# Down-projection weights loaded as four adjacent rows a partition, activations transposed by every fourth column

## The reference

```
def swiglu(h, w1, w3, w2):
    a = silu(einsum('bsd,df->bsf', h, w1)) * einsum('bsd,df->bsf', h, w3)   # 1024 -> 3584
    return einsum('bsf,fd->bsd', a, w2)                                     # 3584 -> 1024, the down projection
```

## Time and profile before

| | |
|---|---|
| median of 3 runs | 1467.38 us (1467.17 to 1470.71) |
| the profiled execution: its own time | 1469.89 us |
| its span, from the first to the last instruction | 1468.1 us |
| PE busy | 1448.4 us (99%), 7542 matmuls |
| DVE busy / ACT busy | 1143.0 us (78%) / 951.2 us (65%) |
| DMA | 439.30 MB, mean 299 GB/s |

### The profile page before, as it was taken

One profiled execution on the slowest core, in us unless ns is written; L12 is line 12 of the kernel. 1 busy time (PEld: TensorE's weight loads), 2 busy tenths in 40 slices (PEclk: granted clock), 3 DMA queues, 4 the chain that ended last, 5 costly groups with the idle time before them and its releaser, 6 DMA issues.

```text
span 1468.1 us, 19713 instructions
## 1 busy us (share of the span) xinstructions
PE 1448.4 (99%) x7542; PEld 1205.7 (82%) x7542; DVE 1143.0 (78%) x968; ACT 951.2 (65%) x844; POOL 35.6 (2%) x22
## 2 busy tenths in 40 slices
PE   8999999999999999999999999999999999999998
PEld 7998888888886788887888888888888888888886
DVE  6984764454476798978888988888898889898886
ACT  7643543443476766767786777777777777677674
POOL 0000000000000000000000001000000000000000
PEclk9999999999999999999999999999999999999999
DMA  9510665544442499999999999999999999999994
GB/s 349 214 58 10 250 216 213 201 171 145 173 163 83 155 362 371 380 358 369 379 359 397 387 367 375 391 364 369 395 391 362 384 375 362 395 390 375 370 370 170
DMA packets 184384, 439.30 MB, mean 299 GB/s; under 512 B 4880, under 2 KB 6416, under 8 KB 184336
## 3 DMA queue, kind: packets, MB, share of 16 engines
q1 hardware_dynamic: 180496, 426.11, 78.6%
q0 software_dynamic: 2848, 10.49, 2.4%
q10 hardware_dynamic: 992, 2.05, 0.4%
HBM read 432.34 MB, written 6.29 MB: 299 GB/s over the span
## 4 chain that ended last, share of the span: by engine, by line
PE 76%; issue 8%; DMA 8%; DVE 6%; ACT 2%; POOL 0%; DVEq 0%; SPq 0%; POOLq 0%; ACTq 0%
PE ps L268 23%; PE ps L270 23%; PE ps L269 23%; DMA raw<-in_od_moe_w 7%; DVE wlo L257 3%; ACT whi L251 1%; PE ps L446 1%; DMA out<-arena,slot_tok 1%; PE ps L974 1%; PE ps L1171 0%; PE ps L873 0%; PE ps L2079 0%; DVE hTlo L312 0%; DVE small L1401 0%; PE ps L329 0%
## 5 line engine op out<-in xcount | busy, mean ns | idle before, releaser
L257 DVE TENSOR_TENSOR wlo<-raw,whi 128x2048 fp32r<-128x2048 f32 x406 | 906.1, 2273 | 167.3 <-ACT whi L251 165.0
L251 ACT CAST whi<-raw 128x2048 fp32r<-128x2048 f32 x406 | 750.7, 1899 | 222.9 <-DMA raw<-in_od_moe_w 162.3
L268 PE MATMUL ps<-whi,hThi 128*128 128x512 f32 (+1 forms) x1240 | 490.1, 395 | 0.0
L270 PE MATMUL ps<-whi,hTlo 128*128 128x512 f32 (+1 forms) x1240 | 482.8, 389 | 0.0
L269 PE MATMUL ps<-wlo,hThi 128*128 128x512 f32 (+1 forms) x1240 | 482.0, 389 | 0.0
L270 PEld LDWEIGHTS ps<-whi,hTlo 128*128 128x128 f32 x1240 | 233.2, 188 | 49.1
L268 PEld LDWEIGHTS ps<-whi,hThi 128*128 128x128 f32 x1240 | 233.5, 188 | 47.5 <-issue 1.2
L269 PEld LDWEIGHTS ps<-wlo,hThi 128*128 128x128 f32 x1240 | 233.6, 188 | 45.7 <-issue 0.2
L268 PE MATMUL ps<-whi,aThi 128*128 128x512 f32 x560 | 219.4, 392 | 0.5 <-DVE wlo L257 0.5
L270 PE MATMUL ps<-whi,aTlo 128*128 128x512 f32 x560 | 218.5, 390 | 0.0
L269 PE MATMUL ps<-wlo,aThi 128*128 128x512 f32 x560 | 218.1, 389 | 0.0
(11 more groups left out here) (308 smaller groups left out, 783.7 us busy)
## 6 DMA issues: line engine op xcount, KB each, us to landing
raw<-in_od_moe_w SPq DMA_DIRECT2D x168, 2048.0 KB, 9.8
raw<-in_ev_ffn_w SPq DMA_DIRECT2D x21, 2048.0 KB, 7.8
raw<-in_ev_w_in SPq DMA_DIRECT2D x6, 2048.0 KB, 12.8
raw<-in_ev_w_out SPq DMA_DIRECT2D x2, 2048.0 KB, 8.6
raw<-in_od_w_in SPq DMA_DIRECT2D x2, 2048.0 KB, 7.8
raw<-in_od_w_out SPq DMA_DIRECT2D x2, 2048.0 KB, 8.1
raw<-in_ev_w_in SPq DMA_DIRECT2D x2, 1024.0 KB, 8.4
xres<-in_x SPq DMA_DIRECT2D x2, 512.0 KB, 4.6
```

Of the source, the lines that this page charges most:

```text
L251: act.copy(whi[s][:, part], raw[s][:, part]).then_inc(hi_ready, 1)
L257: dve.tensor_tensor(wlo[s][:, part], raw[s][:, part], whi[s][:, part].bitcast(F32), ALU.subtract).then_inc(lo_ready, 1)
L268: pe.matmul(to, lhi, rhi, start=first, stop=False)
L270: return pe.matmul(to, llo, rhi, start=False, stop=last)
```

## The change

The rows of a w2 unit are split as (p c) in place of (c p). Partition p then holds rows 4p, 4p+1, 4p+2 and 4p+3, which are one piece of 16 KB in HBM; slice c is rows c, c+4, c+8 and so on. To match, block c of the transposed activations is every fourth column of `actf`, from column c. The transposes read their stationary operand with a step of four elements. Nothing else is changed: the same number of DMAs, bytes, transposes and matmuls, in the same order, with the same waits.

```diff
-        w2f = a["ev_ffn_w2"][0].rearrange("(b c p) n -> b p c n", p=P, c=FC)
+        w2f = a["ev_ffn_w2"][0].rearrange("(b p c) n -> b p c n", p=P, c=FC)
         w1m, w3m = (a[n][0].rearrange("e (k p) n -> e p k n", p=P) for n in ("od_moe_w1", "od_moe_w3"))
-        w2m = a["od_moe_w2"][0].rearrange("e (b c p) n -> (e b) p c n", p=P, c=FC)
+        w2m = a["od_moe_w2"][0].rearrange("e (b p c) n -> (e b) p c n", p=P, c=FC)
...
         def pe_turn(pe, g):
             pe.wait_ge(a_ready, g + 1)
+            by_block = actf.rearrange("p t (i c) -> p t c i", c=FC)
             for c in range(FC):
-                ins = pe.transpose(TP[0][:, c * P:c * P + P], actf[:, 0, c * P:c * P + P], ident)
+                ins = pe.transpose(TP[0][:, c * P:c * P + P], by_block[:, 0, c], ident)
             ins.then_inc(aT_ps, 1)
...
             def turn(i, banks=H1):
 
+                by_block = actf.rearrange("p t (i c) -> p t c i", c=FC)
                 for t in range(TT):
                     pe.wait_ge(a_ready, 2 * i + t + 1)
                     for c in range(FC):
-                        ins = pe.transpose(banks[t][:, c * P:c * P + P], actf[:, t, c * P:c * P + P], ident)
+                        ins = pe.transpose(banks[t][:, c * P:c * P + P], by_block[:, t, c], ident)
                     ins.then_inc(aT_ps, 1)
```

## The result

The changed kernel takes 1476.18 us at the median (21 runs, 1469.0 to 1479.68) against 1467.38 us for the kernel before (21 runs, 1463.8 to 1474.79). The ratio is 1.0041, with a 95% interval of 1.0029 to 1.0053: some 6 us slower (the ratio is that of the means; the medians are 8.8 us apart), where 20.6 us were forecast. That is under a third of the forecast by the ratio and under a half by the medians. Run again beside later experiments it gave 1.0036 (1.0015 to 1.0056) and 1.0048 (1.0034 to 1.0062). The profiled execution took 1473.8 us, its span is 1471.9 us.

A forecast was written before the change was run, and what follows sets the result against it. PE was taken to pace the experts, transfers just behind. 1469.9 us profiled, + 23.9 for strided transpose loads, - 3.0 hidden, 0 for w2 transfers, gave 1490.8, a median of 1488 us since that execution was 2.5 above the median; range 1463 to 1495.

The forecast's parts named there:

- part 2: Transposes' 280 weight loads with a step of four: 0.11 us more for each of 217 bare loads, 23.9 us.
- free groups: Nine transpose groups where PE waits for transfers anyway, 0.33 us each: 3.0 us of the added cost hidden.
- part 1: w2 transfers, 63 DMAs of 128 pieces of 16 KB, not 512 of 4 KB: taken as 0, ends -4.4 and +30 us.
- the stall at 660 to 700 us: In the experts, PE idle 0.73 and 1.89 us in two slices, its lead used up by a chain through transfers.
- all that faster transfers can give back: PE idle plus a slower clock from 660 to 700 us: about 4.4 us recoverable in mid-kernel.
- the chain's 17.45: Experts from 530.95 us: eight rounds of transfer, ACT and DVE at 17.45 us each, 0.67 more than PE's 16.8.
- 217 bare loads: Transpose weight loads no long matmul covers: three in each of 56 expert groups, seven in each of 7 dense groups.
- the span of 512 columns at the moving operand's rate: Strided transpose loads: 512 contiguous moving columns pass in 0.23 us, about 0.12 more than now, hence a doubling.
- Rival 4: 16 KB pieces land later in the experts, 45 steps 0.67 us longer: 30 us, 1497 us without transposes' cost; chance 0.08.
- rival 1: Transposes' weight load does not mind the step, w2 transfers give 0 to 2 us: 1466 us; chance 0.28.
- Rival 2: Load does not mind the step and w2 lands early enough to relieve the eight chain rounds: 1462 us; chance 0.11.
- Rival 3: Transposes' load runs over the whole span, 0.44 us, 0.33 more for each of 217: 1549 us; chance 0.06.

The follow-up runs named there:

- slack_before: The kernel before with half of each w3 unit in the experts not loaded, so transfers are never late: 1464.09 us, ratio 0.9976 to the kernel before.
- slack_after: The changed kernel with half of each w3 unit in the experts not loaded: 1466.58 us, ratio 0.9990 to the kernel before.
- loads_gap: Against the kernel before: four adjacent w2 rows a partition, 16 bytes apart in `raw` (four 4 KB pieces), transposes of adjacent columns: 1470.39 us, 1.0005; repeated 1468.19 us, 1.0003.
- thin_16k: Against the kernel before: one of three matmuls left out, w2 in 16 KB pieces, transposes of adjacent columns: 1374.23 us, ratio 0.9338.

## Why the prediction was wrong

The sign was right, the size was not: 1488 us forecast, 1476.2 measured, inside the range of 1463 to 1495, but the cost is 6 us by the ratio (8.8 by the medians) where 20.6 were named. That the range holds it is luck in good part: part 2 was set some 18 us too high, after its 3.0 us of free groups, and part 1 by 3 to 6 us too low, so two errors partly cancelled. The range was also added up wrongly: 0.08 to 0.13 us a load, with the free groups counted or not, give 1482 to 1496 us, not 1480 to 1493.

- **What bounds the kernel**: right. PE paces the experts with the transfers just behind; slack_before shows that without late transfers the kernel would take 1464 us. But I read the stall at 660 to 700 us as a feature of that place. It was one draw: in the changed kernel's profile those 40 us are clean, and the stall stands at 1011 to 1050 us. The "4.4 us, all that faster transfers can give back" was near the truth (2.5 to 4.6 us over the floor) by luck, as one sample; by the length of the steps that sample had lost 6.4 us, since PE counts as busy in part of a late step. And 16.8 us is only the shortest step: in slack_before two of an expert's seven steps last 17.3 and 17.7 us and the mean is 17.0, so the chain's 17.45 was behind PE by less than 0.67.
- **Part 2, the failed step**: "I take a doubling, 0.11 more for each bare load". It is 0.012 more. The count of 217 bare loads and the first load hidden under its matmul were right, and 217 x 0.012 = 2.6 us is what slack_after minus slack_before gives (2.5). The bound that I leaned on, the span of 512 columns at the moving operand's rate, does not describe how a step is read: the distance of bare loads is the same with steps of 2 and 4, which span 256 and 512 columns, and with a step of 8, which spans 1024, it is back at 0.109 us. The Trainium skill (Advanced Engine Details and Errata, section SBUF Cachelines) says that at least two hits in a 16 byte line are needed to hide the memory's latency. Read as a sufficient number, it would make a step of two float32 free, and it makes a step of eight no better than four; here 0.12 us for two and four and 0.109 for eight don't agree with it. The Trainium skill's price of a weight load (TensorE: Matmul & The Clock Gate, section LDWEIGHTS), 107 ns for 128 columns and silent on steps, is within 12% of the 0.120 us measured.
- **What hides part of it**: the 3.0 us for nine free groups were not there as a block. That a longer PE step gives the transfers room shows at most in the sum: the halves alone bring 1.0015 and 1.0039, together 1.0036 to 1.0048, and the intervals don't tell these from a plain sum.
- **Part 1, the term set to 0**: it is 3 to 6 us, as much as part 2 measured or more. I compared landings of lone loads, 7.6 and 7.8 us, and concluded that a piece's size is indifferent. The lone landing is the wrong gauge: in loads_gap w2 lands latest when alone (8.7 to 8.8 us) and the loss is least. What the runs show in its place is the loss itself, when w2's pieces grow to 16 KB while the transfers are just in time; how the length of the piece makes the landings late stays open. Rival 4 named this effect, "pieces of 16 KB land later" with no cover at a DMA share of 1.02, and gave it 0.08 and 30 us; it is real, at a tenth to a fifth of that price.
- **The other rivals**: rival 1 (the load does not mind the step) came closest on part 2, 0.012 us a load being nearer to nothing than to 0.11, and failed by that small cost and by part 1: 1466 us, and 1476.2 measured. Rival 2 failed with both, as nothing came back. Rival 3 is off by a factor of nearly thirty a load (0.33 us and 0.012).

## What to carry to other kernels

Where an operand's read changes its pattern and no row shows it, a factor of two by analogy is a guess: put the point forecast nearer to the cheap end. The loads here overlap, so what counts is the distance of their starts, not the duration on record. Where transfers are just in time, the longest piece need not be the best, even though its throughput is: measure the whole kernel, not a load that is alone on the queue. And a stall seen once in a profile is a draw: a twin of the kernel with some bytes left out shows the floor, and here it measured a cost of 2.5 to 3 us that the full kernel's spread of 10 to 13 us nearly hid.

## What the runs showed of the hardware

A stationary operand of 128 float32 columns loads in 0.109 us with adjacent columns and with a step of eight, in 0.119 to 0.122 us with steps of two and four (the first bare load of an expert's group excepted, 0.108), though the record of one load grows from 140 ns to 189 at a step of eight and 203 to 208 at two and four. Packets of 2, 4, 8 and 16 KB take 84, 159, 309 and 611 ns at the median: 9 ns each, and 37.6 ns a KB. With w2 in pieces of 16 KB on an otherwise idle queue, the first engine lands earlier (6.8 us after the issue in place of 7.2) and the last later (8.4 in place of 7.8); with the same rows in spaced pieces of 4 KB it is 7.4 and 8.8, so this spread goes with the rows' place more than with the pieces. It is not the whole of it: in thin_16k three such loads, alone on the queue too and with the same rows and pieces (at 228, 251 and 273 us), land after 7.7 to 7.8 us. The kernel before, with a DMA share of 1.02 in the experts, spreads over 10 to 13 us from run to run; slack_before and slack_after, with 0.88, over 2.3 and 2.9 us.
